# A bias table over distances: filled by POOL as runs of equal buckets, where a product with a 0/1 matrix made it

## The chip, the core and the metric

The kernel runs on one core of one Trainium2 chip. The metric is the device time of one execution in microseconds, the median of several runs. The engines are named as in the profile: PE (TensorE matmul), PEld (its weight loads), DVE (VectorE), ACT (ScalarE), POOL (GpSimd) and SP (SyncE, which issues DMAs here).

## The reference

One decoder layer for 512 tokens of 1024 features, all in float32: a half-weighted SwiGLU feed-forward, a mixer with two kinds of attention (sparse with compressed, selected and sliding-window branches; dilated over three strides), and another half-weighted feed-forward. A learned table `rel_bias` of 32 buckets x 20 heads is added to every attention logit, by the bucket of the distance between query and key:

```python
def t5_bucket(dist):
    max_exact = REL_BUCKETS // 2
    d = jnp.maximum(dist, 0)
    df = jnp.maximum(d, max_exact).astype(jnp.float32)
    large = max_exact + (jnp.log(df / max_exact) / math.log(REL_MAX_DIST / max_exact)
                         * (REL_BUCKETS - max_exact)).astype(jnp.int32)
    large = jnp.minimum(large, REL_BUCKETS - 1)
    return jnp.where(d < max_exact, d, large)

    x = x + 0.5 * rms_norm(swiglu(rms_norm(x, ffn1_norm_pre[l]), ffn1_w_gu[l], ffn1_w_down[l]),
                           ffn1_norm_post[l])
    ...
    dist_c = t[:, None] - cmp_end[None, :]
    s_c = s_c + tab[t5_bucket(dist_c)].transpose(2, 3, 0, 1)
    ...
    bias = rel_tab[t5_bucket(jnp.asarray(dist * dilation, jnp.int32))].transpose(2, 0, 1)
```

The buckets depend on the shapes alone and are known when the kernel is built. Neighbouring distances mostly have the same bucket.

## The kernel before

Each engine has its own program, written out by hand, and engines meet at semaphores. Weights come through a ring of two slots. For each weight step SP issues two DMAs of 512 KB into `ring_raw` (L426), ACT rounds them to `ring_hi` (L609), DVE subtracts for the remainder `ring_lo` (L826), and PE multiplies hi x hi, lo x hi and hi x lo (L1257). A step of the up projection is 48 such matmuls of 128x512. Step n of the ring may be loaded once `ring_lo` of step n - 2 is there, and rounded once PE is through with step n - 2.

The kernel starts with four loads of x by token (`x_tok`, L419). PE turns them (L1385), DVE copies them to `xres` (L917), ACT and DVE make `xn_hi` and `xn_lo` (L634, L843), and in the middle of that DVE makes `ring_lo` of step 0. Then the 22 steps of the first up projection follow. The first two, `up(0, 0)` and `up(0, 1)`, stand outside the loop; here they are called steps 0 and 1. After each step DVE and ACT make two operands out of the sums in PSUM, `hT_hi` (L667) and `hT_lo` (L881).

Beside this the bias is prepared. All distances that any of the attention kinds needs lie side by side in one row of 2560 columns, `bias_vec`, one partition for each of the 20 heads, negated, with 1e30 where a column is masked. Before the change it is made so:

- POOL loads the table (`tab`, 32x20, L509) and a 0/1 matrix of 33x2560 (`onehot_sb`, 330 KB, L510), whose last row marks the masked columns. DVE writes the value for them into row 33 of `tab`.
- PE multiplies the two in five pieces of 512 columns (L1354), two behind step 0 and three behind step 1.
- ACT copies each piece out of PSUM, times -1, into `bias_vec` (L679).
- POOL stores `bias_vec` to HBM (L528), waits for it, and issues five DMAs that replicate the rows (L536), 5.4 MB together. Attention reads them back much later.

`bias_vec` lies at 68 KB of an area whose part from 44 KB on is `hT_lo`, so DVE waits for the store (`dve.wait_ge(vec_stored, 16)`, L894) behind step 1, before it enters the loop.

Of the kernel before, what the change touches and what calls it, by code (L numbers as in the profile page):

```python
# [19 lines left out]

# [51 lines left out]
BIAS_PARTS = ((0, 1), (2, 3, 4))  # L72
BIAS_BANKS = (4, 5, 6, 4, 5)
# [22 lines left out]
def bucket(d):  # L96
    d = np.maximum(d, 0)
    exact = BUCKETS // 2
    large = exact + (np.log(np.maximum(d, exact).astype(np.float32) / np.float32(exact))
                     / np.float32(math.log(MAX_DIST / exact)) * (BUCKETS - exact)).astype(np.int32)  # L100
    return np.where(d < exact, d, np.minimum(large, BUCKETS - 1))


def bucket_table():

    i = np.arange(TAB_W)
    dist = np.zeros(TAB_W, np.int64)
    keep = np.ones(TAB_W, bool)
    a = i[NSA_AT:CMP_AT] - NSA_AT
    dist[NSA_AT:CMP_AT] = S - 1 - a  # L110
    dist[CMP_AT:D0_AT] = np.arange(CMP_W) - (CMP_ZERO)
    d0 = DIL_KEYS - 1 - np.arange(D0_W)
    dist[D0_AT:D1_AT] = d0
    keep[D0_AT:D1_AT] = d0 <= P
    d1 = P - 1 - np.arange(D12_W)
    dist[D1_AT:D2_AT] = 4 * d1
    dist[D2_AT:TAB_W] = 4 * d1
    keep[D2_AT:TAB_W] = d1 % 4 == 0
    keep &= dist >= 0
    out = np.zeros((BUCKETS + 1, TAB_W), np.float32)  # L120
    out[bucket(dist), i] = keep
    out[BUCKETS] = ~keep
    return out
# [33 lines left out]
def layer_kernel(nc, x, g1_pre, w1_gu, w1_down, g1_post, gm_pre, w_in, pos_k, cw1_k, cw2_k,  # L157
                 pos_v, cw1_v, cw2_v, w_bn, w_bd, w_out, gm_post, g2_pre, w2_gu, w2_down, g2_post,
                 rel, onehot, out):
    DIL, CMP, NSA = units()  # L160
    NDU, NNU = len(DIL), len(NSA)
# [31 lines left out]
    onehot_sb = at("onehot_sb", R + 56 * K, [TAB_W])  # L193
# [79 lines left out]
    tab = small("tab", [20])  # L273
# [31 lines left out]
    consts, vec_mm, vec_copied, vec_stored = sem("consts"), sem("vec_mm"), sem("vec_copied"), sem("vec_stored")  # L305
    tab_ready, rows_stored = sem("tab_ready"), sem("rows_stored")
# [106 lines left out]
    with block:  # L413
# [84 lines left out]
        def _(pool):  # L498
# [10 lines left out]
            pool.dma_start(tab[0:BUCKETS, :], rel).then_inc(small_loaded, 16)  # L509
            pool.dma_start(onehot_sb[0:BUCKETS + 1, :], onehot).then_inc(small_loaded, 16)  # L510
# [16 lines left out]
            pool.wait_ge(vec_copied, 5)  # L527
# [74 lines left out]
        def _(act):  # L602
# [54 lines left out]
            def ffn(base, pair0, h0, p):  # L657
# [17 lines left out]
                for u in range(2):  # L675
                    up(0, u)
                    for c in BIAS_PARTS[u] if p == 0 else ():
                        act.wait_ge(vec_mm, c + 1)
                        act.activation(bias_vec[0:20, c * S:c * S + S], ps[0:20, BIAS_BANKS[c], :], ACT.Copy,  # L679
                                       scale=-1.0).then_inc(vec_copied, 1)  # L680
# [128 lines left out]
        def _(dve):  # L809
# [99 lines left out]

            dve.memset(tab[BUCKETS:BUCKETS + 1, :], -MASKED).then_inc(tab_ready, 1)  # L910
# [333 lines left out]
        def _(pe):  # L1244
# [70 lines left out]
            def ffn(base, pair0, h0, p, norm):  # L1315
# [27 lines left out]
                for u in range(2):  # L1343
                    up(0, u)
                    if p == 2:
                        x_by_token(2 * u)
                    if p == 0:

                        pe.wait_ge(small_loaded, 32)
                        pe.wait_ge(tab_ready, 1)  # L1350
                        for c in BIAS_PARTS[u]:
                            if c >= 3:
                                pe.wait_ge(vec_copied, c - 2)
                            pe.matmul(ps[0:20, BIAS_BANKS[c], :], tab[0:BUCKETS + 1, :], onehot_sb[0:BUCKETS + 1, c * S:c * S + S],  # L1354
                                      start=True, stop=True).then_inc(vec_mm, 1)
# [4 lines left out]
                if p == 0:  # L1360
                    pe.wait_ge(vec_copied, 5)
                else:
                    pe.wait_ge(xf_copied, 2 * NT)
# [347 lines left out]
```

## Time and profile before

| | us |
|---|---|
| median of 3 runs | 1268.86 |
| lowest, highest | 1268.37, 1269.44 |
| the profiled execution, its own time | 1270.22 |
| span of the profiled execution | 1268.5 |

One execution was profiled. Its span is from the first to the last instruction. The busy shares say how much of the span each engine works. The chain of waits goes back from the end, at each step to what released it, and tells which engine's work set the time at each moment. The timeline gives single instructions with their start, so that two starts can be subtracted; PE's matmuls overlap, so their durations can't be added. A row of a timeline names in brackets how long the engine stood idle before it and what ended that.

### The profile page before, as it was taken

How to read it: one execution, taken by the hardware profiler on the slowest of the kernel's cores; microseconds unless marked ns; L12 is line 12 of the kernel's file. 1: busy time of each engine (PE TensorE's matmuls, PEld its weight loads, DVE VectorE, ACT ScalarE, POOL GpSimd, SP SyncE). 2: the span in 40 equal slices, each digit the busy share in tenths (PEclk: the TensorE clock that was granted, in tenths of full speed). 3: DMA queues.
4: the chain of work that ended last, by engine and by line, in shares of the span. 5: the costliest groups of instructions: out<-in, count | busy, mean ns of one | idle time of the engine just before them, and what ended most of it. 6: DMA issues, size and time to landing. Idle time of an engine off the chain costs nothing.

```text
span 1268.5 us, 15806 instructions
## 1 busy us (share of the span) xinstructions
PE 1232.9 (97%) x6204; PEld 1025.7 (81%) x6204; DVE 578.8 (46%) x863; ACT 402.4 (32%) x608; POOL 83.8 (7%) x90
## 2 busy tenths in 40 slices
PE   8999999999998999999999999999999999999997
PEld 7788888888886788996877888887788888888886
DVE  4444444432227435336788443653644444442113
ACT  4322222221126112236554322344432222221113
POOL 0100000000006600000020000001600000000000
PEclk8999999999999999999999999999999999999999
DMA  6573333322231633462200033332233333322211
GB/s 178 152 227 99 97 93 87 95 100 92 97 100 34 183 108 99 134 199 67 70 2 2 1 100 100 100 97 70 67 98 90 89 91 95 99 100 99 99 67 67
DMA packets 140651, 121.91 MB, mean 96 GB/s; under 512 B 4091, under 2 KB 129211, under 8 KB 140555
## 3 DMA queue, kind: packets, MB, share of 16 engines
q1 hardware_dynamic: 136736, 108.02, 28.0%
q0 software_dynamic: 3712, 13.26, 3.4%
q8 instruction: 29, 0.48, 0.2%
q14 instruction: 14, 0.11, 0.0%
q10 hardware_dynamic: 160, 0.04, 0.0%
HBM read 116.86 MB, written 8.90 MB: 99 GB/s over the span
## 4 chain that ended last, share of the span: by engine, by line
PE 89%; POOL 4%; DVE 3%; ACT 2%; DMA 1%; issue 1%; POOLq 0%; SPq 0%; DVEq 0%; ACTq 0%
PE ps L1257 51%; PE ps L1336 18%; PE ps L1430 4%; PE ps L1664 3%; PE ps L1525 3%; POOL xres L515 2%; POOL acc L523 2%; PE ps L1484 2%; PE ps L1648 2%; PE ps L1495 2%; PE ps L1636 1%; DMA x_tok<-in_x 1%; DVE pT_sb L1042 1%; PE ps L1270 1%; DVE ring_lo L832 1%
## 5 line engine op out<-in xcount | busy, mean ns | idle before, releaser
L1257 PE MATMUL ps<-xn_hi,ring_hi 128*128 128x512 f32 x992 | 390.0, 393 | 8.0 <-DVE xn_lo L843 4.6
L1257 PE MATMUL ps<-xn_hi,ring_lo 128*128 128x512 f32 x992 | 386.8, 390 | 0.0
L1257 PE MATMUL ps<-xn_lo,ring_hi 128*128 128x512 f32 x992 | 386.6, 390 | 0.0
L826 DVE TENSOR_TENSOR ring_lo<-ring_raw,ring_hi 128x2048 fp32r<-128x2048 f32 (+1 forms) x93 | 213.1, 2294 | 242.6 <-ACT ring_hi L609 242.6
L609 ACT ACTIVATE ring_hi<-ring_raw 128x2048 fp32r<-128x2048 f32 (+1 forms) x93 | 173.7, 1870 | 255.4 <-PE ps L1336 166.6
L1257 PEld LDWEIGHTS ps<-xn_hi,ring_hi 128*128 128x128 f32 x992 | 186.6, 188 | 52.7 <-issue 6.6
L1257 PEld LDWEIGHTS ps<-xn_hi,ring_lo 128*128 128x128 f32 x992 | 186.5, 188 | 39.5
L1257 PEld LDWEIGHTS ps<-xn_lo,ring_hi 128*128 128x128 f32 x992 | 186.7, 188 | 37.6
L1336 PE MATMUL ps<-hT_hi,ring_lo 128*128 (+1 forms) x352 | 136.9, 389 | 0.0
L1336 PE MATMUL ps<-hT_hi,ring_hi 128*128 (+1 forms) x352 | 136.9, 389 | 0.0
L1336 PE MATMUL ps<-hT_lo,ring_hi 128*128 (+1 forms) x352 | 136.9, 389 | 0.0
L661 ACT ACTIVATE silu_g<-silu_g 128x512 f32<-128x512 f32 x44 | 27.8, 632 | 329.6 <-DVE silu_g L872 329.6
L872 DVE TENSOR_TENSOR silu_g<-ps,rb 128x512 f32<-128x512 f32 x44 | 30.4, 691 | 197.8 <-PE ps L1257 197.8
L1336 PEld LDWEIGHTS ps<-hT_lo,ring_hi 128*128 128x128 f32 x352 | 66.1, 188 | 13.8
L1336 PEld LDWEIGHTS ps<-hT_hi,ring_lo 128*128 128x128 f32 x352 | 66.1, 188 | 13.8
L1336 PEld LDWEIGHTS ps<-hT_hi,ring_hi 128*128 128x128 f32 x352 | 66.1, 188 | 13.5
L1525 PE MATMUL ps<-v_all,pT_sb 128*128 128x128 f32 (+1 forms) x440 | 59.4, 278 | 6.0 <-DVE pT_sb L1042 4.7
L515 POOL TENSOR_TENSOR xres<-xres,ysb 128x512 f32<-128x512 f32 x16 | 25.4, 1622 | 553.4 <-DVE ysb L857 553.4
L1525 PEld LDWEIGHTS ps<-v_all,pT_sb 128*128 128x128 f32 x440 | 54.2, 193 | 8.4 <-DVE pT_sb L1042 6.4
L754 ACT ACTIVATE p_sb<-s_sb,stat_m 128x512 f32<-128x512 f32 (+3 forms) x64 | 35.6, 556 | 43.1 <-DVE stat_m L1029 39.4
L1042 DVE COPY pT_sb<-ps 128x512 f32<-128x512 f32 (+2 forms) x60 | 39.5, 660 | 8.1 <-PE ps L1495 6.4
L1430 PE MATMUL ps<-ring_hi,xn_hi 128*128 128x256 f32 x128 | 36.5, 285 | 2.7 <-DVE ring_lo L832 2.7
(247 smaller groups left out, 1213.3 us busy)
## 6 DMA issues: line engine op xcount, KB each, us to landing
ring_raw<-in_ffn_w_gu SPq DMA_DIRECT2D x88, 512.0 KB, 5.0
ring_raw<-in_ffn_w_down SPq DMA_DIRECT2D x44, 512.0 KB, 3.6
ring_raw<-in_w_in SPq DMA_DIRECT2D x44, 512.0 KB, 4.7
ring_raw<-in_w_out SPq DMA_DIRECT2D x8, 512.0 KB, 4.1
bias_rows_sparse<-bias_by_distance POOLq DMA_DIRECT2D x1, 2560.0 KB, 13.6
x_tok<-in_x SPq DMA_DIRECT2D x4, 512.0 KB, 5.9
ring_raw<-in_cmp_w_k SPq DMA_DIRECT2D x4, 512.0 KB, 4.3
ring_raw<-in_cmp_w_v SPq DMA_DIRECT2D x4, 512.0 KB, 7.2
```

The costliest lines, as they stand in the source:

```text
L515: pool.tensor_tensor(xres[:, m, :], xres[:, m, :], ysb[:, m, :], ALU.add).then_inc(x_new_pool, 1)
L609: e = act.activation(dst, src, ACT.Copy)
L661: act.activation(silu_g[:, u, :], silu_g[:, u, :], ACT.Silu).then_inc(act_read, 1)
L754: e = act.activation(p_sb[:, u % 2, c0:c1], s_sb[:, u % 2, c0:c1], ACT.Exp, bias=least, scale=-1.0, accum_out=den)
L826: e = dve.tensor_tensor(dst, src, f32(r), ALU.subtract)
L872: dve.tensor_tensor(silu_g[:, u, :], ps[:, 2 * slot, :], rb[:, :], ALU.mult).then_inc(g_scaled, 1)
L1042: dve.tensor_copy(pT_sb[:, u % 2, 0:w], ps[:, 4 + u % 2, 0:w]).then_inc(pT_ready, 1)
L1257: e = pe.matmul(ps[:, 2 * (slot if pair is None else pair) + c, :], part(a, slot, k * 256 + c * P, P), xn[b][:, k, :], start=(k == 0 and i ...
L1336: e = pe.matmul(ps[:, m, :], part(a, n0 % 2, kk * D + m * P, P), hT[b][:, at_k], start=(start and kk == 0 and q == 0), stop=(stop and kk = ...
L1430: e = pe.matmul(ps[:, pair + t // 2, (t % 2) * 256:(t % 2) * 256 + 256], xn[b][:, k, tokens], part(a, n % 2, k * 256, 256), start=(k == 0 ...
L1525: e = pe.matmul(ps[:, bank, o0 - before:o0 + HD + after], pT_sb[:, u % 2, x * P:x * P + P], vj, start=(j == 0), stop=(j == len(v) - 1))
L1664: e = pe.matmul(ps[:, 2 * i + c, :], part(a, n % 2, k * 256 + c * P, P), xn[b][:, k, :], start=(k == 0 and q == 0), stop=(k == KD - 1 and ...
```

## The change

POOL fills `bias_vec` alone. The host sends `rel_bias` transposed (20x32), and POOL loads it into `tab`, one head for each partition. It sets all 2560 columns to 1e30, negates the table into `neg_tab`, and then, for each run of columns with the same bucket, copies the one column of `neg_tab` over the run, spread by a step of zero. The list of runs is made when the kernel is built; in the part for stride 16 every fourth column counts, and the runs have a step of 4. Two semaphores order the memset, the multiply and the copies. The store, its wait and the replication are as they were, and DVE waits for the store at the same place. The 0/1 matrix, its load, the five matmuls, the five copies by ACT and DVE's memset are gone.

```diff
@@ the list of runs, made on the host
-    out = np.zeros((BUCKETS + 1, TAB_W), np.float32)
-    out[bucket(dist), i] = keep
-    out[BUCKETS] = ~keep
-    return out
+    of = bucket(dist)
+    runs = []
+    for first, end, step in ((NSA_AT, CMP_AT, 1), (CMP_AT, D0_AT, 1), (D0_AT, D1_AT, 1), (D1_AT, D2_AT, 1), (D2_AT, TAB_W, 4)):
+        at = [int(j) for j in i[first:end] if keep[j]]
+        for b, group in itertools.groupby(at, key=lambda j: int(of[j])):
+            group = list(group)
+            assert group == list(range(group[0], group[0] + step * len(group), step))
+            runs.append((b, group[0], step, len(group)))
+    return runs
@@ POOL
-            pool.dma_start(tab[0:BUCKETS, :], rel).then_inc(small_loaded, 16)
-            pool.dma_start(onehot_sb[0:BUCKETS + 1, :], onehot).then_inc(small_loaded, 16)
+            pool.dma_start(tab[0:20, :], rel).then_inc(small_loaded, 16)
+            pool.memset(bias_vec[0:20, :], MASKED).then_inc(vec_filled, 1)
...
-            pool.wait_ge(vec_copied, 5)
+            pool.wait_ge(small_loaded, 16)
+            pool.tensor_scalar(neg_tab[0:20, :], tab[0:20, :], -1.0, None, ALU.mult).then_inc(tab_negated, 1)
+            pool.wait_ge(tab_negated, 1)
+            pool.wait_ge(vec_filled, 1)
+            for b, first, step, n in RUNS:
+                e = pool.tensor_copy(bias_vec[0:20, first:first + step * (n - 1) + 1:step], neg_tab[0:20, b:b + 1].broadcast_to([20, n]))
+            e.then_inc(vec_filled, 1)
+            pool.wait_ge(vec_filled, 2)
             pool.dma_start(vec_dram, bias_vec[0:20, :]).then_inc(vec_stored, 16)
@@ ACT
-                    for c in BIAS_PARTS[u] if p == 0 else ():
-                        act.wait_ge(vec_mm, c + 1)
-                        act.activation(bias_vec[0:20, c * S:c * S + S], ps[0:20, BIAS_BANKS[c], :], ACT.Copy,
-                                       scale=-1.0).then_inc(vec_copied, 1)
@@ DVE
-            dve.memset(tab[BUCKETS:BUCKETS + 1, :], -MASKED).then_inc(tab_ready, 1)
@@ PE
-                    if p == 0:
-
-                        pe.wait_ge(small_loaded, 32)
-                        pe.wait_ge(tab_ready, 1)
-                        for c in BIAS_PARTS[u]:
-                            if c >= 3:
-                                pe.wait_ge(vec_copied, c - 2)
-                            pe.matmul(ps[0:20, BIAS_BANKS[c], :], tab[0:BUCKETS + 1, :], onehot_sb[0:BUCKETS + 1, c * S:c * S + S],
-                                      start=True, stop=True).then_inc(vec_mm, 1)
...
-                if p == 0:
-                    pe.wait_ge(vec_copied, 5)
-                else:
+                if p:
                     pe.wait_ge(xf_copied, 2 * NT)
```

How the instructions stand in a row shows two places. The first is PE between step 1 and the loop that starts with step 2 (the branch and the register rows are the loop's entry). Before:

```order
L1257 MATMUL ps<-xn_hi,ring_lo 128x512
L1354 MATMUL ps<-onehot_sb,tab 20x512 x3
L1356 UNCONDITIONAL_BRANCH
L1356 ISA
L1319 REGISTER_ALU
L1257 MATMUL ps<-xn_hi,ring_hi 128x512
```

With the change, whose lines have other numbers (L1263 is the matmul that was L1257):

```order
L1263 MATMUL ps<-xn_hi,ring_lo 128x512
L1353 UNCONDITIONAL_BRANCH
L1353 ISA
L1325 REGISTER_ALU
L1263 MATMUL ps<-xn_hi,ring_hi 128x512
```

The three products are gone and nothing else moved; the same holds for the two between steps 0 and 1. The second place is POOL, from the load of the table to the store. Before:

```order
L507 AFFINE_SELECT valid<-valid 128x1
L509 DMA tab<-in_rel_bias 32x20
L510 DMA onehot_sb<-bucket_of_distance 33x2560
L528 DMA bias_by_distance<-bias_vec 20x2560
L536 DMA bias_rows_sparse<-bias_by_distance 1024x1x640
```

With the change (L537 are the copies; the first runs of the row are shown, `x32` stands for 32 copies of one column each):

```order
L514 DMA tab<-in_rel_bias 20x32
L515 MEMSET bias_vec 20x2560
L533 TENSOR_SCALAR neg_tab<-tab 20x32
L537 COPY bias_vec<-neg_tab 20x62
L537 COPY bias_vec<-neg_tab 20x118
L537 COPY bias_vec<-neg_tab 20x86
...
L537 COPY bias_vec<-neg_tab 20x1 x32
...
L540 DMA bias_by_distance<-bias_vec 20x2560
```

In all 107 copies stand between the multiply and the store, and the store no longer stands behind anything that PE or ACT does.

## Rows read from the trace of the kernel before

**Rows 1.** The page, busy time and share of the span of each engine.

```profile
PE 1232.9 (97%) x6204; PEld 1025.7 (81%) x6204; DVE 578.8 (46%) x863; ACT 402.4 (32%) x608; POOL 83.8 (7%) x90
```

**Rows 2.** Chain of waits, 0 to 130 us: start us, us, what.

```profile
2.21 10.61 DMA x_tok<-in_x
...
34.32 1.82 PE ps L1354 x4
...
47.26 2.68 PE ps L1354 x6
```

**Rows 3.** Timeline of DVE, 16 to 22 us: start, us, instruction.

```profile
16.55 0.75 DVE L843 SCALAR_TENSOR_TENSOR xn_lo<-xres,gains,xn_hi 128x512 fp32r<-128x512 f32 x1
...
19.73 2.29 DVE L826 TENSOR_TENSOR ring_lo<-ring_raw,ring_hi 128x2048 fp32r<-128x2048 f32 x1
```

**Rows 4.** Timeline of PE between step 0 and step 1.

```profile
33.69 0.39 PE L1257 MATMUL ps<-xn_lo,ring_hi 128*128 128x512 f32 x1
33.92 0.40 PE L1257 MATMUL ps<-xn_hi,ring_lo 128*128 128x512 f32 x1
...
36.07 0.50 PE L1257 MATMUL ps<-xn_hi,ring_hi 128*128 128x512 f32 x1
36.41 0.39 PE L1257 MATMUL ps<-xn_lo,ring_hi 128*128 128x512 f32 x1
```

**Rows 5.** Timeline of PE between step 1 and step 2.

```profile
46.87 0.39 PE L1257 MATMUL ps<-xn_hi,ring_lo 128*128 128x512 f32 x1
...
49.87 0.50 PE L1257 MATMUL ps<-xn_hi,ring_hi 128*128 128x512 f32 x1
```

**Rows 6.** Timeline of DVE, 31 to 72 us, [idle before].

```profile
31.03 2.29 DVE L826 TENSOR_TENSOR ring_lo<-ring_raw,ring_hi 128x2048 fp32r<-128x2048 f32 x1 [1.24 <-ACT ring_hi L609]
...
61.29 0.69 DVE L872 TENSOR_TENSOR silu_g<-ps,rb 128x512 f32<-128x512 f32 x1 [7.91 <-PE ps L1257]
...
64.48 2.29 DVE L826 TENSOR_TENSOR ring_lo<-ring_raw,ring_hi 128x2048 fp32r<-128x2048 f32 x1 [1.11 <-ACT ring_hi L609]
...
71.97 0.69 DVE L872 TENSOR_TENSOR silu_g<-ps,rb 128x512 f32<-128x512 f32 x1 [4.59 <-PE ps L1257]
```

**Rows 7.** The page's groups, ACT's rounding: count, busy us, mean ns, idle before.

```profile
L609 ACT ACTIVATE ring_hi<-ring_raw 128x2048 fp32r<-128x2048 f32 (+1 forms) x93 | 173.7, 1870 | 255.4 <-PE ps L1336 166.6
```

**Rows 8.** DMA, 0 to 13 us: packets, MB, share of engines; issues: KB, us to landing.

```profile
q0 software_dynamic: 96, 0.34, 10.9%
...
onehot_sb<-bucket_of_distance POOLq DMA_DIRECT2D x1, 330.0 KB, 9.4
...
tab<-in_rel_bias POOLq DMA_DIRECT2D x1, 2.5 KB, 6.0
```

**Rows 9.** Timeline of PE, 9 to 14 us.

```profile
12.86 1.54 PE L1385 MATMUL ps<-ident,x_tok 128*128 128x128 f32 x6 [3.22 <-DMA x_tok<-in_x]
```

**Rows 10.** Busy times of 8 to 13 us; last: granted clock, DMA share, GB/s.

```profile
8.00:13.00 5.00, 1.07 (x6) 0.61 (x6) 0.17 (x1) 0.00 (x0) 0.00 (x0) 0.81 1.13 235
```

**Rows 11.** Timeline of POOL, 1 to 2 us.

```profile
1.10 0.10 POOL L501 MEMSET eps<- 128x1 f32 x1
1.14 0.10 POOL L502 MEMSET valid<- 128x1 f32 x1
...
1.72 0.18 POOL L507 TENSOR_SCALAR_AFFINE_SELECT valid<-valid 128x1 f32<-128x1 f32 x1
```

**Rows 12.** The instructions of L595: ns min/median/max, first and last start.

```profile
L595 POOL TENSOR_TENSOR o_dil<-o_dil,c_p x8: 609/610/611, 657.3 to 661.3; 128x256 f32<-128x256 f32 x8
```

**Rows 13.** The same of L843, at 10:30 and 895:900, and of L826, 890:902.

```profile
L843 DVE SCALAR_TENSOR_TENSOR xn_lo<-xres,gains,xn_hi x8: 742/744/746, 16.5 to 25.8; 128x512 fp32r<-128x512 f32 x8
...
L843 DVE SCALAR_TENSOR_TENSOR xn_lo<-xres,gains,xn_hi x2: 1454/1456/1458, 895.0 to 896.7; 128x512 fp32r<-128x512 f32 x2
...
L826 DVE TENSOR_TENSOR ring_lo<-ring_raw,ring_hi x1: 3376/3376/3376, 898.1 to 898.1; 128x2048 fp32r<-128x2048 f32 x1
```

**Rows 14.** Time to landing: the replication (L536), then L426 in 64:70.

```profile
DMA to landing us min/median/max: 13.6/15.9/21.0
...
DMA to landing us min/median/max: 11.9/13.3/14.7
```

More of the change, by code:

```diff
@@ L21 @@
+import itertools
 import math
@@ L71 @@
 assert TAB_W == 5 * S
-BIAS_PARTS = ((0, 1), (2, 3, 4))
-BIAS_BANKS = (4, 5, 6, 4, 5)
 CMP_ZERO = CB - 1 + CS * (CPAD - 1)
@@ L101, in bucket, with bucket_runs @@
     return np.where(d < exact, d, np.minimum(large, BUCKETS - 1))
-def bucket_table():
+def bucket_runs():
     i = np.arange(TAB_W)
@@ L158, in layer_kernel @@
                  pos_v, cw1_v, cw2_v, w_bn, w_bd, w_out, gm_post, g2_pre, w2_gu, w2_down, g2_post,
-                 rel, onehot, out):
+                 rel, out):
     DIL, CMP, NSA = units()
+    RUNS = bucket_runs()
     NDU, NNU = len(DIL), len(NSA)
@@ L192, in layer_kernel @@
     x_sq = at("x_sq", R + 28 * K, [KD, S])
-    onehot_sb = at("onehot_sb", R + 56 * K, [TAB_W])
     bias_vec = at("bias_vec", R + 68 * K, [TAB_W])
@@ L272, in layer_kernel @@
     rstd = small("rstd", [NT])
-    tab = small("tab", [20])
+    tab = small("tab", [BUCKETS])
+    neg_tab = small("neg_tab", [BUCKETS])
     posT = small("posT", [2, 16])
@@ L304, in layer_kernel @@
     small_loaded, gains_loaded, x_sums = sem("small_loaded"), sem("gains_loaded"), sem("x_sums")
-    consts, vec_mm, vec_copied, vec_stored = sem("consts"), sem("vec_mm"), sem("vec_copied"), sem("vec_stored")
-    tab_ready, rows_stored = sem("tab_ready"), sem("rows_stored")
+    consts, vec_filled, vec_stored = sem("consts"), sem("vec_filled"), sem("vec_stored")
+    tab_negated, rows_stored = sem("tab_negated"), sem("rows_stored")
     xT_done = sem("xT_done")
@@ L1700 @@
         a = np.ascontiguousarray(inputs[name])
-        if name != "rel_bias":
-            a = a[0]
+        a = np.ascontiguousarray(a.T) if name == "rel_bias" else a[0]
         arrays[f"in_{name}"] = a
-    arrays["bucket_of_distance"] = bucket_table()
     for name, a in arrays.items():
```

## The prediction, made before the changed kernel was run

> **What bounds the kernel now.** I read the page first, for the busy shares: PE is busy 97% of the span, DVE 46%, ACT 32%, POOL 7% [rows 1]. So the default is that time is PE's, and an edit on another engine counts only where PE waits for it. The chain of waits over the first 130 us then shows the place of this change: from 12.86 us on it is all PE, and two of its pieces are the product with the 0/1 matrix, 1.82 us at 34.32 and 2.68 us at 47.26 [rows 2]. They lie between steps 0 and 1 and between steps 1 and 2 of the first up projection. Ahead of PE's work stands one DMA wait, 10.61 us for the last x_tok load [rows 2]. Between the two is a stretch in which DVE decides: step 0 can't start before its ring_lo, which ends at 19.73 + 2.29 = 22.02 [rows 3].
>
> **Part 1, PE: the five products go.** The trace has ten matmuls for them, two passes each (x4 and x6 in [rows 2]). They overlap, so busy time is the wrong measure, and I use starts. L1257 matmuls in a row start 0.23 us apart. At the first place the last one of step 0 starts at 33.92 and the first of step 1 at 36.07: 2.15 us, of which 0.23 would remain, so 1.92; the second then starts 0.34 behind and not 0.23, another 0.11 for filling again. Sum 2.03 us [rows 4]. At the second place 46.87 to 49.87 is 3.00, less 0.23, plus the same 0.11: 2.88 us [rows 5]. Together **4.91 us**. The order of PE's instructions shows the rows gone, and nothing in their stead.
>
> Is something else late when they are gone? Step 1 could start at 33.92 + 0.23 = 34.15. Its ring_lo (DVE, at 31.03) ends at 33.32 [rows 6]: 0.83 us of margin. Step 2 could start 10.9 later (48 x 0.227), at 45.0; its ring_hi may start when step 0 ends, and hi and lo take 1.9 + 2.3 [rows 6, 7], so it is there near 38.6, 6.4 of margin. So all 4.91 us come through, and what is behind is the same row of PE work moved forward.
>
> **Part 2, ACT and DVE** lose five copies out of PSUM and a memset of one row. At 32% and 46% [rows 1], with work that follows PE's steps, that is worth 0.
>
> **Part 3, DMA: the 330 KB of the 0/1 matrix are not loaded.** It takes 9.4 us to landing from 2.75 us on, so it is in flight together with the last x_tok load, for which PE stands still 3.22 us, up to 12.86 [rows 8, 9]. In the first 13 us queue 0, which is this load and the 2.5 KB table, has 10.9% of 16 engines' time: 0.109 x 13 = 1.42 us on each engine; the share of the engines in 8 to 13 us is 1.13, that is, full [rows 8, 10]. So x_tok lands between 0 and 1.4 us earlier. I take **0.9**: the engines are full, but the ring loads that share them can take part of the room. What follows (transposes, DVE's copies, ring_lo, the start of step 0) moves along.
>
> **Part 4, POOL: 107 copies, a memset and a multiply.** The bucket runs are 107, over 1,298 columns; the other columns are the memset's. The table lands at 2.04 + 6.0 = 8.0 [rows 8], the multiply takes perhaps 0.4 with its waits, the copies start at 8.4. The trace has no small copy on POOL, so the price has bounds. Below: memsets of one column start 0.04 us apart: 107 x 0.04 = 4.3 us. Above: L595, two inputs of 256 columns, at 0.61 us for each copy, whatever its length: 65.3 us. The nearest row is the affine_select of 128x1, one column read and one written: 0.18 us. With 2.2 ns a column from L595 ((661.3 - 657.3)/7 = 0.57 us from start to start, over 256) that is 107 x 0.18 + 1298 x 0.0022 = 22.1 us [rows 11, 12]. I take 0.18, since an average copy has 12 columns. The fill is then over at 30.5, and the store, at the 3.4 us that it takes now, at 34.
>
> The Trainium skill (Perfetto Trace Analysis, GPSIMD Engine Instruction) says that a recorded span on GpSimd is unreliable and that starts should be compared. The trace agrees: the one-column memset reads 0.10 us, and two start 0.04 apart [rows 11]. By that rule 0.18 is rather too much, and the fill is over sooner; it changes no term of the sum.
>
> Who waits? DVE, behind its step 1, before it may write the part of hT_lo that lies on the vector. Its next work is due at the end of step 2, 61.29 now, 61.3 - 5.4 = 55.9 then: 22 us of cover. Behind that PE has more: DVE's ring_lo at 64.48 ends at 66.77, and PE needs it when step 3 ends, at 71.97 [rows 6], 5.2 us. So PE loses time only if the store lands after 55.9 + 5.2 = 61.1, that is, if the fill ends after 57.7: (57.7 - 8.4)/107 = **0.46 us for each copy**. Queued behind the copies on POOL are only the store and the five replications, whose readers come hundreds of us later. Cost taken: 0.
>
> **Part 5, POOL against DVE.** Beside POOL, DVE is slower in instructions with two inputs in SBUF: xn_lo takes 744 ns in the start and 1,456 beside POOL's additions, ring_lo 2.29 us alone and 3,376 ns [rows 3, 13]. Ahead of step 0 three xn_lo and one ring_lo lie on the path (16.55 to 22.02) [rows 3], in the time of the fill. Bounds: 0 (the fill over before 16, or too few columns read to matter) and 3 x 0.71 + 1.09 = 3.2 us. Those of [rows 13] are POOL at 512 columns and two inputs, a copy here reads 12. I take **0.4**, near the lower end. On ring_lo of step 1 the margin of 0.83 covers most of 1.09.
>
> The Trainium skill (SBUF — State Buffer, Who interferes with whom) says more strictly that a VectorE instruction with two SBUF inputs and a GpSimd instruction that reads SBUF exclude each other for the whole instruction. By it each of the four DVE instructions waits for at most one running copy, 4 x 0.18 = 0.7 us as an estimate, and the sum below would be 5.1 us instead of 5.4.
>
> **Part 6, the replication comes earlier.** After the store five DMAs from POOL, landing after 13.6 to 21.0 us, fill the DMA engines, from 56 us on now, from 34 then. A ring load among them took 14.7 us at most [rows 14]. The load for step 3 is issued when ring_lo of step 1 is done, 33.3 - 0.5, and may land at 47.5; with 4.2 for hi and lo the result is there at 51.7, and PE wants it at 45.0 - 0.5 + 10.9 = 55.4. If the fill were over by 18, the load for step 2 (issued at 22.0 - 0.5, the second half 0.6 later) would be in it: landing 36.8, result 41.0, wanted 44.5. Cost 0 in both.
>
> **Sum.** 4.9 + 0.9 - 0.4 = 5.4 us. Against the profiled execution's own span of 1268.5 us that is 1263.1; its time was 1270.22, the median of the three runs is 1268.86, and carried to the median the sum gives **1263.5 us**.
>
> **Rivals.** (a) POOL slows the start to its upper bound: 4.9 + 0.9 - 3.2 = 2.6, 1266.3. For it: xn_lo at 1,456. Against: 12 columns a copy. (b) x_tok lands no earlier, the rest as forecast: 4.9 - 0.4 = 4.5, 1264.4. For it: the ring loads take the room. (c) **Slower**: a copy on POOL has a fixed price of several tenths. From 0.46 us on PE waits before step 4 for DVE, which waits for the store; from 0.46 + 5.4/107 = 0.51 the kernel is slower than before. At L595's 0.61 the fill ends at 8.4 + 65.3 = 73.7, 16.0 past 57.7: 1268.9 - 5.4 + 16.0 = 1279.5. For it: no row bounds a small copy from above. Against: 0.18 and 0.04 in [rows 11]. (d) An early fill, and the replication holds a ring load as long as the longest of its own, 21.0: landing at 43.1, result for step 2 at 47.3, 2.8 late: 1266.3. (e) The products are gone, but PE waits as long for something else there: about 1268.4. Against: the margins of 0.83 and 6.4.
>
> **How the numbers follow.** Forecast together with (b), which lies in its range: 0.76; (a) 0.09; (c) 0.07; (d) 0.05; (e) 0.03. The bounds of parts 3 and 5 alone give 1268.9 - 4.9 - 1.4 = 1262.6 to 1266.3. The low end goes to 1262.2, since behind a shorter standstill PE and DVE may close up their small gaps; the high end to 1266.6 takes in (a) and (d). A measurement of this kernel can tell 0.2%, 2.5 us. Faster by more (under 1266.3): 0.76, half of (a), half of (d), 0.83. Within: the other halves, (e) and the part of (c) with a price near 0.5: 0.11. Slower: the rest of (c), 0.06.
>
> **What would show it.** Right: no gap between L1257 matmuls near 33 and 44 us; copies on POOL less than 0.25 us from start to start and the store before 40; PE's wait for x_tok over at 12 or sooner. Part 5 is read from xn_lo and ring_lo ahead of step 0: 0.74 and 2.29 where POOL doesn't matter. Wrong: DVE waiting for the store beyond 56 us and PE for ring_lo near 66 (c); ring_hi waiting for a DMA near 34 or 46 with a PE wait behind it (d); ring_lo of step 0 over later than 22.0 (a); a PE wait between steps 0 and 1 (e).

## The result

| | us |
|---|---|
| changed kernel, median of 6 runs | 1261.91 (1261.37 to 1264.36) |
| kernel before, median of 6 runs | 1269.63 (1268.37 to 1271.19) |
| ratio, 95% interval | 0.9941, 0.9929 to 0.9954 |
| the profiled execution, its own time | 1264.36 |
| its span | 1262.5 |

The change makes the kernel faster by 7.7 us in 1269.6 between the medians, 7.5 by the ratio. Measured again later, beside nine runs of the kernel before, the ratio is 0.9924 (0.9911 to 0.9938) at a median of 1261.96. The forecast was 1263.5 in a range of 1262.2 to 1266.6. The sign held, and so did the largest term, the products; the term of the load was too small by three quarters, and 1261.91 lies 0.3 us below the range. The profiled execution is the slowest of its six: its start has gained 9.06 us, and its span is only 6.0 us shorter than that of the profiled execution before. The 3.05 us between the two are taken up at the end.

The page's busy line, against [rows 1]. PE has ten matmuls less, POOL 108 instructions more:

```profile
PE 1228.0 (97%) x6194; PEld 1025.6 (81%) x6194; DVE 578.7 (46%) x862; ACT 399.7 (32%) x603; POOL 108.0 (9%) x198
```

The chain of waits over the first 125 us (start us, us, what), against [rows 2]:

```profile
2.21 7.36 DMA x_tok<-in_x
...
10.06 2.48 DVE xres L923 x4
...
15.72 2.21 DVE ring_lo L834
17.93 0.04 issue
17.98 5.74 PE ps L1263 x24
...
28.83 96.37 PE ps L1263 x425
```

The two pieces of the products are gone and nothing stands in their place. The first piece is shorter too: the last x_tok load holds PE until 9.57 and not 12.82. The timeline of DVE shows what came of it, against [rows 3] and [rows 6]:

```profile
14.99 0.73 DVE L851 SCALAR_TENSOR_TENSOR xn_lo<-xres,gains,xn_hi 128x512 fp32r<-128x512 f32 x1
15.64 2.28 DVE L834 TENSOR_TENSOR ring_lo<-ring_raw,ring_hi 128x2048 fp32r<-128x2048 f32 x1
...
52.23 0.69 DVE L880 TENSOR_TENSOR silu_g<-ps,rb 128x512 f32<-128x512 f32 x1 [5.00 <-PE ps L1263]
```

The end of step 2 has moved from 61.29 to 52.23. With step 0's start (22.07 before, 17.98 now) and the end of x_tok's wait between, the 9.06 us fall into three parts: 3.25 up to the end of the wait; (22.07 - 12.82) - (17.98 - 9.57) = 0.84 from there to step 0; and (61.29 - 22.07) - (52.23 - 17.98) = 4.97 in steps 0 to 2.

Busy times of 13 to 18 us (PE, PEld, DVE, ACT, POOL; last: granted clock of TensorE, DMA share, GB/s), before:

```profile
13.00:18.00 5.00, 5.00 (x24) 5.00 (x25) 4.14 (x7) 3.49 (x5) 0.00 (x0) 0.50 0.99 264
```

and with the change:

```profile
13.00:18.00 5.00, 3.85 (x36) 3.66 (x34) 5.00 (x7) 3.44 (x4) 5.00 (x15) 1.00 0.55 135
```

Before, after PE's standstill of 3.22 us [rows 9], the transposes ran at the lower level, 1.2 GHz. With the change PE's idle time ahead of the last x_tok was 1.07 us and the clock stayed at 2.4 GHz. The timeline of POOL:

```profile
8.40 0.31 POOL L533 TENSOR_SCALAR neg_tab<-tab 20x32 f32<-20x32 f32 x1 [3.39 <-DMA tab<-in_rel_bias]
8.77 22.21 POOL L537 COPY bias_vec<-neg_tab 20x62 f32<-20x62 f32 x107
31.28 0.59 POOL L540 DMA_DIRECT2D bias_by_distance<-bias_vec  x1 [0.30 <-POOL bias_vec L537]
35.77 0.88 POOL L548 DMA_DIRECT2D bias_rows_sparse<-bias_by_distance  x1 [3.91 <-DMA bias_by_distance<-bias_vec]
```

The 107 copies took 22.2 us and the store had landed by 35.8, 16 us before DVE's work at the end of step 2 needs it.

### The profile page after: what moved, and what is told of

It reads as the page before. It is cut to its first block, busy times and chain, and to the rows that moved or that the text cites. A ratio compares the mean times of both kernels' runs of the same rounds, so it can differ in the third digit from the quotient of the medians.

```text
span 1262.5 us, 15887 instructions
## 1 busy us (share of the span) xinstructions
PE 1228.0 (97%) x6194; PEld 1025.6 (81%) x6194; DVE 578.7 (46%) x862; ACT 399.7 (32%) x603; POOL 108.0 (9%) x198
## 4 chain that ended last, share of the span: by engine, by line
PE 88%; POOL 4%; DVE 4%; ACT 2%; issue 1%; DMA 1%; POOLq 0%; SPq 0%; DVEq 0%; ACTq 0%
PE ps L1263 51%; PE ps L1342 18%; PE ps L1425 4%; PE ps L1659 3%; PE ps L1520 3%; POOL xres L520 2%; POOL acc L528 2%; PE ps L1479 2%; PE ps L1643 2%; PE ps L1490 2%; PE ps L1631 1%; DVE pT_sb L1048 1%; PE ps L1276 1%; DMA x_tok<-in_x 1%; DVE ring_lo L840 1%
## 5 line engine op out<-in xcount | busy, mean ns | idle before, releaser
L1263 PE MATMUL ps<-xn_hi,ring_hi 128*128 128x512 f32 x992 | 390.1, 393 | 9.0 <-DVE xn_lo L851 4.6
L1263 PE MATMUL ps<-xn_hi,ring_lo 128*128 128x512 f32 x992 | 387.9, 391 | 0.0
L1263 PE MATMUL ps<-xn_lo,ring_hi 128*128 128x512 f32 x992 | 387.7, 391 | 0.0
L1263 PEld LDWEIGHTS ps<-xn_hi,ring_hi 128*128 128x128 f32 x992 | 187.4, 189 | 51.0 <-DVE ring_lo L834 5.1
L1263 PEld LDWEIGHTS ps<-xn_hi,ring_lo 128*128 128x128 f32 x992 | 187.1, 189 | 39.5
L1263 PEld LDWEIGHTS ps<-xn_lo,ring_hi 128*128 128x128 f32 x992 | 187.3, 189 | 38.1
```

The lines of the kernel that those rows point to most:

```text
L1263: e = pe.matmul(ps[:, 2 * (slot if pair is None else pair) + c, :], part(a, slot, k * 256 + c * P, P), xn[b][:, k, :], start=(k == 0 and i ...
```

## Experiments

Every kernel here still computes the whole result; extra loads, copies, additions and matmuls go to places that nobody reads. "Start" below means the time of the first silu_g after step 2, 61.29 before and 52.23 after.

### One part alone: the load out of x_tok's way, the products kept

The kernel before, with the load of the 0/1 matrix issued only when all of x_tok is there:

```diff
+            for t in range(NT):
+                pool.wait_ge(x_loaded[t], 16)
             pool.dma_start(onehot_sb[0:BUCKETS + 1, :], onehot).then_inc(small_loaded, 16)
```

> The kernel before, with one edit: POOL issues the load of the 0/1 matrix only when all four x_tok loads have landed. The five products stay. My theory now (the load of 330 KB holds the last x_tok load back by 3.25 us, and the standstill behind it lowers PE's clock, 0.84 us more until step 0): x_tok's wait ends at 9.6 us, ring_lo of step 0 at 18.0, the gaps of 2.0 and 2.9 us for the products stay, and the time is 4.1 us below before (about 1265). The term as I predicted it: x_tok at 11.9, time 0.9 below before. A rival, that x_tok landed early for another reason than this load (POOL's own work, one execution's luck): x_tok at 12.8 and the time of before.

Measured: 1266.62 against 1270.36 us, ratio 0.9958 (0.9944 to 0.9972). Its chain of waits:

```profile
2.21 7.32 DMA x_tok<-in_x
...
15.68 2.21 DVE ring_lo L828
...
30.20 1.82 PE ps L1356 x4
32.02 11.12 PE ps L1259 x48
43.14 2.68 PE ps L1356 x6
```

The products are there in full, and the wait for x_tok is as short as in the changed kernel. Start 57.17: 4.12 us of the 9.06 are the load's, 4.94 the products'. The time went down by 3.7. This one run shows that the term I had put at 0.9 is nearer 4.

Single executions scatter here, and the kernels of this document give 15 traces to see by how much. Without such a load beside it, and with the ring loads issued as here, the last x_tok load has landed at 8.67 to 9.68 (nine traces), on average 9.25; with the 330 KB on partitions 0 to 32 beside it at 11.1 to 12.82 (six traces), on average 12.1. The two groups don't touch, so the load is the cause. Its price up to the end of the wait is 2.8 us on average. The 3.25 of the pair of traces above sets the highest of the second group against a high one of the first.

### The reverse: the changed kernel with the 330 KB loaded again

```diff
             pool.dma_start(tab[0:20, :], rel).then_inc(small_loaded, 16)
+            pool.dma_start(onehot_sb[0:BUCKETS + 1, :], onehot).then_inc(extra_loaded, 16)
             pool.memset(bias_vec[0:20, :], MASKED).then_inc(vec_filled, 1)
...
+            pool.wait_ge(extra_loaded, 16)
             pool.dma_start(vec_dram, bias_vec[0:20, :]).then_inc(vec_stored, 16)
```

> The changed kernel, with a load of the same 330 KB to the same 33 partitions put back at the place where the 0/1 matrix was loaded (its data is not used). This is the change without its DMA part. If the load is the cause: x_tok at 12.8, ring_lo of step 0 ends at 22.0, PE's granted clock 0.5 around 13 to 17 us, and only the products' 4.9 us are saved: about 1264.3. If it is not: x_tok at 9.6 and the time of the changed kernel, 1261.9. POOL's share in slowing DVE, if there is any, shows in xn_lo over 0.74 and ring_lo over 2.29.

Measured: 1273.02 us, ratio 1.0001 (0.9975 to 1.0027), but in two groups: four of ten executions at 1264.2 to 1266.6, six at 1272.3 to 1275.6. The profile fell on a low one (span 1263.0). There x_tok's wait ends at 12.57 and start is 56.05: 3.8 us of the gain lost, near the 4.1 of the first experiment. It doesn't explain the high group. A second time, to have one of that in a profile:

> The kernel of e2 once more, for its trace. Its times fell in two groups, 1264 to 1266 and 1272 to 1276. In e2's trace, of the faster group, ring_hi of step 4 waited 3.5 us for its ring load, which had been issued just behind the start of the replication, and PE had 0.96 us left. If the slower group comes from that load, a trace of it shows ring_hi waiting 5 us or more there and PE waiting for ring_lo before step 4. If it comes from the start, x_tok's wait ends later than 12.6.

Measured: 1274.29 us (1265.72 to 1276.19), ratio 1.0015 (0.9994 to 1.0036), and the profiled execution is of the high group, at 1273.91. Its chain of waits from 20 us on:

```profile
33.31 24.75 DMA ring_raw<-in_ffn_w_gu
58.06 0.02 issue
58.08 1.92 ACT ring_hi L625
60.00 0.02 issue
60.02 2.31 DVE ring_lo L838
```

and its timeline of PE:

```profile
62.37 0.79 PE L1267 MATMUL ps<-xn_hi,ring_hi 128*128 128x512 f32 x1 [6.66 <-DVE ring_lo L838]
```

A ring load for step 3, issued at 33.3, was under way for 24.75 us; the median of the 88 loads of this kind in this trace is 5.0. Its company were the replications, issued from 32.48 on. This is the mechanism of rival (d), at step 3 and not at step 2, and with a longer hold than the 21.0 of [rows 14]. PE stood still 6.66 us, and 60 to 65 us ran at a granted clock of 0.50. In the low trace the replication came at 33.70, between the two halves of the same ring load, issued at 33.24 and 33.79, and these landed after 4.2 and 6.2 us; the two halves for step 4 took 19.6 and 21.8 us, and PE's row of matmuls has no gap. To show it by taking the company away, the same kernel with the replication held until PE is through with step 2:

```diff
             pool.wait_ge(vec_stored, 16)
+            pool.wait_ge(w_used, 3)
```

> e2 with one more wait: POOL issues the five DMAs of the replication only when PE is through with step 2 (56 us), as late as in the kernel before, not at 33.7. If the slower group of e2 comes from the replication meeting the ring loads, it is gone, and all times are 1264 to 1266. If it comes from x_tok in the start, the two groups stay.

Measured: 1265.38 us (1264.92 to 1265.64), ratio 0.9961 (0.9947 to 0.9976). The high group, 12 of the 18 executions above, is gone in all four, and the median is 8.9 us lower, so the meeting of the replication and a ring load was the cause. That it hangs on the order of the two within a microsecond is read from the two traces alone. What is left against the kernel before, measured on the same chip at 1270.29, is 4.9 us: the products alone, with the load still in x_tok's way. Part 1 had 4.91.

### Why 330 KB weigh so much: bytes or place

The changed kernel with the load put back, the same bytes now over 128 partitions:

```diff
+            pool.dma_start(onehot_sb[:, 0:660], onehot.rearrange("a b -> (a b)").rearrange("(p c) -> p c", p=P)).then_inc(extra_loaded, 16)
```

> As e2, but the same 330 KB go to 128 partitions of 2.6 KB each instead of 33 partitions of 10 KB. If the bytes are what delays x_tok (all 16 DMA engines are full), x_tok lands as late as in e2, 12.8. If it is their being packed on 33 partitions, or few long rows on few engines, x_tok lands between 9.6 and 10.6 (330 KB at the 300 to 370 GB/s of this stretch are 0.9 to 1.1 us) and the time is 1262 to 1263.

Measured: 1263.54 us, ratio 0.9941 (0.9924 to 0.9958), start 52.50. And 32 rows of 10 KB as before, but on every fourth partition:

```diff
+            pool.dma_start(onehot_sb[0:P:4, :], onehot[0:BUCKETS, :]).then_inc(extra_loaded, 16)
```

> As e2 (the changed kernel with a load beside x_tok), but 32 rows of 10 KB go to every fourth partition, 0 to 124, instead of the first 33. Rows, their length and their number are those of e2, the place is as wide as in e3. e2's x_tok landed at 12.57, e3's at 9.77. If it is the place (33 neighbouring partitions are reached through few ports), x_tok lands near e3's: 9.6 to 10.2. If it is the long rows, few for each engine, x_tok lands near e2's: 12 or later.

Measured: 1262.69 us (two runs), ratio 0.9946 (0.9928 to 0.9964), start 52.65. The chain's first piece and the load's queue in 0 to 13 us (packets, MB, share of 16 engines' time), first of the load on partitions 0 to 32:

```profile
2.21 10.35 DMA x_tok<-in_x
...
q0 software_dynamic: 96, 0.34, 10.6%
```

spread over 128:

```profile
2.21 7.56 DMA x_tok<-in_x
...
q0 software_dynamic: 112, 0.34, 6.9%
```

and on every fourth:

```profile
2.21 7.77 DMA x_tok<-in_x
...
q0 software_dynamic: 80, 0.33, 6.5%
```

Against the 9.57 of the changed kernel's trace the same 0.33 MB cost x_tok 3.0 us, 0.2 and 0.4; against the average of 9.25 it is 3.3, 0.5 and 0.7. Neither the bytes nor the length of a row does it. What is left is that the 33 rows lie on partitions 0 to 32, or that there are 33 of them. Their packets also take more engine time, 10.6% (8.6 to 10.9% over the six traces) against 6.5% for nearly as many bytes. The Trainium skill (SBUF — State Buffer, Door 1: The DMA port swizzle) states that a transfer's bandwidth depends on how many of 16 ports its partitions reach, that partitions 0 to 31 reach eight and all 128 sixteen; by its table every fourth partition reaches all sixteen too. These three traces agree. But the number of rows isn't separated from their place: the last kernel has 32 rows and the first 33, and the Trainium skill (DMA: Bandwidth & Descriptors, Why a DMA increments its semaphore by 16 and not by 1) has the number of engines for a transfer depend on the count of rows. A load of 32 rows to partitions 0 to 31 would have told the two apart; it wasn't run.

### The half clock ahead of step 0

The kernel before, with matmuls on constants ahead of PE's last wait for x_tok; first 36 of them, then 12 (shown):

```diff
                     if m == 0:
+                        if t == 3:
+                            keep_warm(12, 6)
                         pe.wait_ge(x_loaded[t], 16)
```

> The kernel before, with 36 matmuls of the identity put in front of PE's wait for the fourth x_tok load, so that PE works while it would stand still. x_tok still lands at 12.8. If the low granted clock behind the standstill (0.5 from 11.5 to 17.5 us) is what made DVE's copies start later and with gaps, the clock stays 1.0 and ring_lo of step 0 ends 0.8 us sooner, 21.2, time 0.8 below before. If the clock had no share, ring_lo ends at 22.0 and the time is that of before.

Measured: 1273.9 us, ratio 1.0028 (1.0018 to 1.0038). The 36 took 8.04 us and outlasted the wait: DVE's first copy came at 16.08. So the size was wrong; but from there to the end of ring_lo it took 7.87 us, and 8.57 in the kernel before.

> The kernel before with 12 matmuls of the identity ahead of PE's wait for the fourth x_tok load (in e5 there were 36, and PE was busy with them 3 us longer than the wait, so that DVE's copies began at 16.1). 12 take 2.7 us at full clock, less than the wait. DVE's first copy then comes at 13.3 to 13.5 as before. If the half clock cost what I think, ring_lo of step 0 ends 7.9 us after that copy as in e5 and in the changed kernel, at 21.2 to 21.4, not 8.6 after it, and step 1's start moves with it: 0.7 us off the time of before.

Measured: 1269.37 against 1269.16 us, ratio 0.9999 (0.9988 to 1.0011). The granted clock was 1.00 in 10 to 18 us, and first copy to end of ring_lo again 7.87, as in the changed kernel (10.06 to 17.93). So the low clock costs 0.70 us in the trace, most of the 0.84. In the time it doesn't show: the interval is 2.9 us wide, and here it rules out a gain over 1.5.

### Two and three copies for one

The price of a copy decides rival (c). Each run copied also to a spare place, once more (shown; `range(2)` for twice more):

```diff
             for b, first, step, n in RUNS:
+                for i in range(1):
+                    pool.tensor_copy(scratch[0:20, i, first:first + step * (n - 1) + 1:step], neg_tab[0:20, b:b + 1].broadcast_to([20, n]))
                 e = pool.tensor_copy(bias_vec[0:20, first:first + step * (n - 1) + 1:step], neg_tab[0:20, b:b + 1].broadcast_to([20, n]))
```

> The same with every copy made twice, 214 copies: the fill ends at 8.8 + 44.4 = 53.2 and the store lands at 57.7, 5.5 us after DVE's work is due and 0.3 after PE would wait. By the cover worked out before, the time is 0 to 1 us over that of the changed kernel though POOL works twice as long. If PE waited for DVE from 52.2 on, the loss would be 5.5 us.

Measured: 1262.42 us, ratio 0.994 (0.9924 to 0.9957).

> The changed kernel, with every copy of POOL made three times (twice into unused room beside the vector), 321 copies. It tests the cover. The 107 copies took 22.2 us; 321 take 66.6, from 8.8 to 75.4, and the store lands 4.5 later, at 80. DVE's work is due at 52.2 and PE waits 5.2 later, at 57.4, so PE stands still some 22.5 us before step 4: about 1284.5. If DVE's wait had more cover than that, or the fill's length mattered in another way (port, DMA), the loss is not 22.5.

Measured: 1276.02 us, ratio 1.0047 (1.003 to 1.0064). DVE's first silu_g after step 2 with three copies:

```profile
68.73 0.69 DVE L883 TENSOR_TENSOR silu_g<-ps,rb 128x512 f32<-128x512 f32 x1 [21.62 <-DMA bias_by_distance<-bias_vec]
```

and PE behind it, ahead of step 4:

```profile
74.34 0.79 PE L1266 MATMUL ps<-xn_hi,ring_hi 128*128 128x512 f32 x1 [11.60 <-DVE ring_lo L837]
```

That silu_g and the next one with two copies:

```profile
55.14 0.69 DVE L883 TENSOR_TENSOR silu_g<-ps,rb 128x512 f32<-128x512 f32 x1 [7.77 <-DMA bias_by_distance<-bias_vec]
...
63.03 0.69 DVE L883 TENSOR_TENSOR silu_g<-ps,rb 128x512 f32<-128x512 f32 x1 [1.81 <-PE ps L1266]
```

With two, the fill ends at 51.3, DVE is 2.9 us late and one step later it waits for PE again: the time is that of the changed kernel. With three the fill ends at 64.9, PE stands still 11.6 us and then runs at a granted clock of 0.51 in 75 to 80 us, and the kernel is slower than before, 13.6 us above the one with two. The mechanism of (c) is real. Part 4's limit of 57.7 for the end of the fill was for a start of 55.9; with one of 52.2 it is 54.0, and the two runs lie on either side of it. But 321 copies took 56.2 us, not three times 22.2. POOL beside DVE with two copies shows why. POOL:

```profile
13.76 0.17 POOL L539 COPY scratch<-neg_tab 20x1 f32<-20x1 f32 x1
13.88 0.73 POOL L540 COPY bias_vec<-neg_tab 20x1 f32<-20x1 f32 x1
14.55 0.17 POOL L539 COPY scratch<-neg_tab 20x1 f32<-20x1 f32 x1
...
15.81 2.26 POOL L539 COPY scratch<-neg_tab 20x1 f32<-20x1 f32 x1
```

and DVE at the same time:

```profile
13.82 0.74 DVE L854 SCALAR_TENSOR_TENSOR xn_lo<-xres,gains,xn_hi 128x512 fp32r<-128x512 f32 x1
...
15.74 2.28 DVE L837 TENSOR_TENSOR ring_lo<-ring_raw,ring_hi 128x2048 fp32r<-128x2048 f32 x1
```

A copy lasts 0.17 us, and free copies start 0.12 apart. A copy beside an xn_lo lasts 0.73, beside a ring_lo 2.26, as long as these do, while DVE's instruction is not slower. So 22.2 us for 107 copies are some 13 of copying and 9 of waiting for DVE.

### POOL against DVE, made as bad as it gets

Ten copies of 512 columns ahead of the fill, and in another kernel eight additions of two inputs of 128x512:

```diff
+            for i in range(10):
+                pool.tensor_copy(scratch[0:20, i, :], neg_tab[0:20, 0:1].broadcast_to([20, S]))
```

> The changed kernel, with ten copies of 20x512 (one input, spread from one column) by POOL into unused room, ahead of the fill, in the time of DVE's xn_lo and ring_lo of the start (from 8.8 us on). If DVE is slowed by the columns that POOL reads, xn_lo goes from 0.74 towards 1.1 to 1.46 and ring_lo from 2.28 towards 3.4, and step 0 starts 1 to 3 us later. If a copy with one input doesn't touch DVE at all, both stay and the time stays 1261.9, the store still landing before 52.

Measured: 1262.65 us, ratio 0.9948 (0.9932 to 0.9964), start 52.60. DVE while the wide copies ran, then after them:

```profile
12.11 1.13 DVE L854 SCALAR_TENSOR_TENSOR xn_lo<-xres,gains,xn_hi 128x512 fp32r<-128x512 f32 x1
...
15.34 0.74 DVE L854 SCALAR_TENSOR_TENSOR xn_lo<-xres,gains,xn_hi 128x512 fp32r<-128x512 f32 x1
```

```diff
+            for i in range(2, 10):
+                pool.tensor_tensor(scratch[:, i, :], scratch[:, 0, :], scratch[:, 1, :], ALU.add)
```

> The same with eight additions of 128x512 with two inputs by POOL in place of the ten copies. These are the form that slowed DVE in the trace of before: I expect xn_lo of 1.1 to 1.46 us and ring_lo of about 3.4 in the start, step 0 starting 1.5 to 3 us later, and a time of 1263.5 to 1265. Where DVE is slowed here and not in e7, what matters is the kind or width of POOL's instruction, not that POOL works.

Measured: 1266.55 us, ratio 0.9967 (0.9951 to 0.9983), start 56.45. DVE beside the additions:

```profile
14.96 1.16 DVE L857 SCALAR_TENSOR_TENSOR xn_lo<-xres,gains,xn_hi 128x512 fp32r<-128x512 f32 x1
16.05 3.35 DVE L840 TENSOR_TENSOR ring_lo<-ring_raw,ring_hi 128x2048 fp32r<-128x2048 f32 x1
```

Rival (a) is a real mechanism, and its price depends on how long the single POOL instruction is: next to nothing beside the fill's own copies (from the first copy to the end of ring_lo the changed kernel takes 7.87 us, the same as the kernel without a fill at full clock above; single xn_lo of other traces read up to 0.84), up to 0.4 on xn_lo with copies of 0.61, 0.4 on xn_lo and 1.07 on ring_lo with additions of 1.7. In the last kernel step 0 starts at 19.41, in spite of an earlier x_tok, and then runs at a granted clock of 0.55 in 18 to 23 us: the first 24 matmuls take 8.48 us where the changed kernel took 5.74, and that is how 1.4 us at step 0 became 4.2 at step 2.

### Can x_tok land still sooner?

The changed kernel, with the ring's early loads held back on SP: first only step 1's, until x_tok is there; then also step 0's, until the second x_tok load is (shown):

```diff
                 if not (isinstance(i, int) and 2 * i + c < 2):
                     sp.wait_ge(lo_ready, 2 * i + (c - 1))
+                else:
+                    sp.wait_ge(x_loaded[NT - 1 if c == 1 else 1], 16)
```

> The changed kernel, with SP issuing the ring load of step 1 only when x_tok has landed. x_tok's 2 MB then share the engines with one ring load and not with two. If they are slowed by the ring loads, x_tok lands before 9.6, by up to 1 us, and all that follows comes as much sooner: 1261 to 1261.9. Step 1's data would be there at about 14, ACT takes it at 24.9. If ring loads queue behind x_tok anyway, nothing moves.

Measured: 1262.23 us, ratio 0.9944 (0.9931 to 0.9958); x_tok's wait ends at 9.46, 0.1 us sooner. Nothing moves.

> As e6, and step 0's ring load waits for the second x_tok load too (some 8 us with two ring loads beside it). x_tok lands sooner still, near 2.2 + 2 MB / 370 GB/s + 1 = 8.7 us, if the ring load of step 0 holds it back; but ACT wants step 0's data at 13.3 less what x gains, and it is issued some 3 us later and lands after 12 or 13: the start gains at most 0.5 us over e6 or loses up to 1.

Measured: 1261.45 us, ratio 0.994 (0.9927 to 0.9954). The first copy comes at 9.12 and step 2 ends at 51.32, 0.9 us sooner than in the changed kernel's trace. That isn't the holding, as far as can be seen: a kernel of the next section without it (e11) ends step 2 at 51.37, x_tok there at 8.67, and one with the same holding (e12) at 52.26, x_tok there at 9.56. Holding the ring loads back isn't shown to gain anything, in the traces or in the time.

### Does the earlier replication cost the changed kernel something?

In the changed kernel the ring load of step 5, whose second half is issued at 47.3, lands 15.7 us later, at 63.0; ring_hi begins on it at 64.17 with no idle time. That is 1.1 us to spare, less than Part 6 saw anywhere. Held back until step 2 is done, alone (e11) and with the holding of the ring loads (e12):

```diff
             pool.wait_ge(vec_stored, 16)
+            pool.wait_ge(w_used, 3)
```

> The changed kernel with the same added wait, so that the replication starts at 52 us. In the changed kernel's trace no ring_hi waits for a DMA in the first 90 us, so PE should lose nothing to the replication either way: 1261 to 1262.5, as without the wait. If the replication did cost the changed kernel a part of what the start gave, this is faster by that part.

Measured: 1261.38 us (1260.79 to 1262.5), ratio 0.9934 (0.9919 to 0.9948).

> e6b (ring loads of steps 0 and 1 held back, x_tok at 8.4) with that wait too: the candidate for the fastest. Start 0.9 us before the changed kernel's, so 1260.5 to 1261.5 where the clock behind 550 us is no different; no ring_hi waits for a DMA in the up projection.

Measured: 1261.84 us (1260.59 to 1264.55), ratio 0.9935 (0.9923 to 0.9947). Then changed kernel and held kernel side by side on one chip:

> The changed kernel itself, beside the version that holds the replication back (the next run), on one chip. In its trace the load for step 5, issued at 46.8, lands 15.7 us later, at 63.0, and ring_hi wants it at 64.17: 1.1 us to spare. If that margin holds in all executions, the two kernels are equal within 0.1%, near 0.9937 of the kernel before. If it is at times used up, as with the load beside it, single executions of this kernel lie 3 us or more above its lowest, those of the next kernel don't, and its median is higher by 1 us or more.

Measured: 1261.96 us (1260.99 to 1262.83), ratio 0.9924 (0.9911 to 0.9938).

> The changed kernel, with the replication issued only when PE is through with step 2 (near 51.7). Margin theory: the same as the changed kernel within 0.1%. Meeting theory: lower by 1 us or more, and without single executions 3 us above the lowest.

Measured: 1261.5 us (1260.9 to 1262.1), ratio 0.9922 (0.9909 to 0.9936). The two are equal: the margin of 1.1 us holds, and no kernel tried here beats the changed one by more than can be measured.

## Why the prediction was right and where it failed

**Part 1, the products, 4.91 us: right.** 4.97 in the two traces, 4.94 by the first experiment's start, 4.9 in time by the run with load and held replication. Starts were the right measure, and nothing was late in the products' place: rival (e) fell.

**Part 3, the load, 0.9 us: the step that failed.** It measured 3.25 up to the end of the wait, 2.8 on the average of all traces, and 0.84 more behind it; in time 3.7 (the load late) and 4.0 (1265.38 against 1261.38, on one chip). I had spread queue 0's share evenly over 16 engines and taken 0.109 x 13 = 1.42 us as an upper bound. It was none: the same bytes on 128 or on every fourth partition would have fitted it, with 0.2 to 0.7 us, and the 33 rows on partitions 0 to 32 didn't. That x_tok is there only when its slowest share is, which a mean over 16 engines doesn't see, is how I explain it; the profile doesn't tell one DMA engine from another. The row that could have warned me was the count of partitions in the load's shape. The second piece, the half clock behind a standstill of 3.22 us, was in view as 0.81 in [rows 10], and I gave it no term; it is 0.70 of the 0.84. Rival (b), x_tok no earlier, erred to the other side.

**Part 5, POOL against DVE, 0.4 us: too high, it is 0.** xn_lo took 0.74 at most and ring_lo 2.28 beside the fill, ahead of step 0. The Trainium skill's rule (SBUF — State Buffer, Who interferes with whom), that the two exclude each other for a whole instruction, is borne out by the copies that lasted 0.73 and 2.26 us; my 0.7 us from it was wrong because the wait fell on POOL's side. With wide instructions the same rule would have one side stop whole, and ring_lo's 3.35 is longer by 1.07 where an addition lasts 1.7.

**Part 4, the fill, over at 30.5: right by luck.** It was over at 31.0, with 107 copies of some 0.12 us and 9 us of waiting, where I had 107 of 0.18. Had the path in front been without DVE's work, it would have ended near 22. The limit of 57.7, or 54.0 with the true start, isn't measured closer than that it lies between the two runs: a fill to 51.3 cost nothing, one to 64.9 made the kernel slower.

**Part 6, the replication, 0: right for this kernel, by less than I thought.** The bound of 14.7 us for a ring load among replications was too low; 15.7, 21.8 and 24.8 were seen. In the changed kernel the replication was issued at 35.8, half a us behind the ring load of step 4, which took 5.6 at most; the next pair had 1.1 us to spare. With the load put back it came, in the high trace, just ahead of a ring load, and that group's cost is in the 8.9 between the medians. Rival (d) had a chance of 0.05 at a price of 2.8; where its mechanism came up, the price was three times that.

**The sum.** 4.9 + 4.1 - 0 = 9.0 at the start by the pair of traces, and 4.9 + 2.8 + 0.7 = 8.4 by the averages, an estimate. The medians of the changed kernel lie 7.7 and 9.5 us below those of the kernel before, in the two times that both were measured, and those of the version with the replication held 8.9 and 10.0. The forecast with Part 3 as it measured would have been 1268.9 - 9.0 = 1259.9, 2 us under the median of 1261.91; from the median of six runs of the kernel before, 1269.63, and with 8.4 it is 1261.2. My low end of 1262.2 came from Part 3's false bound.

What separates the two profiled executions, 9.06 us at the start and 6.0 in the span, is 3.05 us in two stretches, 1.44 between the strided values' store and the load of bias_n, 1.61 between the second addition to x and the output. Neither is the change's. The first stretch took 66.45 us before and 67.89 in the changed kernel, and 65.2 to 66.2 in the 18 other traces, 65.89 in the changed kernel profiled again. The second takes one of two times in all 20 traces, 385.2 to 385.4 us in six and 386.9 to 387.0 in fourteen; both kinds are among the kernels with the products and among those with the fill, and one kernel, the one with fill and load, has shown both in its two traces (385.29 with a granted clock of 1.00 in 902 to 912 us, 386.91 with 0.76 and 0.90 in the matching 910 to 920). The first stretch differs in the clock too. Busy times of 580 to 585 us in the first profiled one:

```profile
580.00:585.00 5.00, 5.00 (x24) 4.78 (x26) 2.56 (x10) 3.35 (x15) 0.00 (x0) 0.50 0.01 3
```

and in the changed kernel profiled again, span 1260.3:

```profile
580.00:585.00 5.00, 5.00 (x40) 4.01 (x39) 3.28 (x15) 3.12 (x15) 0.00 (x0) 0.95 0.01 3
```

Both fell, the second one sooner and for less time (0.71 in 575 to 580 us, where the first had 0.88). PE had waited ahead of it, busy 2.20 and 2.87 us of those 5, but it was busy 2.75 and 2.67 us in two kernels with the replication held, and their clock stayed at 1.00. Why one execution has the fall and another hasn't stays open.

## What to carry to other kernels

When a load shares the DMA engines with one that the first matmul waits for, look at how many partitions it fills and which, not only at its share of the engines: 330 KB on 33 neighbouring partitions cost 2.8 us there on average, the same bytes spread out 0.2 to 0.7. Before an effect below a microsecond in the start is read from one pair of traces, look how far traces of the same start lie apart: here it was up to 1 us. Small POOL work may stand beside a busy DVE for nothing, if POOL has the time to wait for it. When a step moves earlier, reckon for the bulk transfers behind it which load they now meet: here a microsecond of order between a replication and a ring load was worth 8.9 us.

## What was new of the hardware

- A load of 0.33 MB from POOL on partitions 0 to 32 took 8.6 to 10.9% of 16 DMA engines' time in 13 us, and 6.5% on every fourth partition; an x_tok load beside it landed 2.8 us later on average in the one case, 0.4 to 0.7 in the other.
- POOL copies of a few columns, read with a step of zero, start 0.12 us apart; one of 20x512 takes 0.61.
- Beside a VectorE instruction with two SBUF inputs a short POOL copy lasts as long as that instruction (0.73, 2.26 us), which is slowed little or not at all (xn_lo 0.73 to 0.84, 0.74 to 0.75 without POOL); wide POOL instructions slow it: xn_lo from 0.74 to 1.16, ring_lo from 2.28 to 3.35.
- A 512 KB load, 5.0 us in the median, took 24.8 when issued 0.8 us behind the first of 5.4 MB of copies from HBM to HBM, and 6.2 when issued 0.1 us behind it.
